# Second block's values and forget gate from split operands, and a reordered first block, in a two-block transformer kernel

## The reference, cut to what matters

```python
def reference(...):        # 512 tokens, width 1024
    x = first_block(x, mem, ...)     # one hybrid layer
    return second_block(x, ...)

def hybrid_layer(x, mem, ...):
    h = rmsnorm(x, norm_g);  proj = h @ w_in        # latents, conv parts, q_mem, gates, r
    q, k, v from rmsnorm(latents)                   # 8 heads, rope on the last 32 of 96
    o_attn = attention(q, k, v) * silu(g_attn)
    o_conv = c_b * short_conv(c_c * c_u) * silu(g_conv)
    mkv = rmsnorm(mem, mem_norm_g) @ w_mkv          # 256 memory rows
    o_mem = attention(rmsnorm(q_mem), rmsnorm(m_k), m_v) * silu(g_mem)   # 4 heads
    y = sum of sigmoid(r + b) * (o @ w_br) over the three branches
    return x + y @ w_out

def second_block(x, ...):
    xn = rms_norm(x, norm1_g);  proj = xn @ w_in    # fq fk fv, forget, dq dk dv
    8 causal heads with forget gates, 8 dilated heads; h = x + mixed @ w_out
    h = h + peer_ffn(rms_norm(h))                   # 16384 experts, top 16 of 8 heads
    return rms_norm(h)
```

## Time and profile before

| | |
|---|---|
| three runs | 2448.0, 2450.22, 2455.33 us; median 2450.22 us |
| the profiled execution | 2454.08 us, of which the span is 2452.2 us |
| PE matmul busy | 2312.9 us, 94% of the span |
| POOL, DVE, ACT busy | 1226.3, 1252.9, 898.9 us |
| mean granted PE clock | 0.978 of full speed |

### The profile page before, as it was taken

The page is one execution under the profiler, slowest core; times in us unless marked ns, Lnnn a source line. Parts: engine busy times, 40 slices in busy tenths (PEclk is TensorE's granted clock), DMA queues, the critical chain, the costliest instruction groups (busy, mean ns, idle before and its releaser), DMA issues.

```text
span 2452.2 us, 29634 instructions
## 1 busy us (share of the span) xinstructions
PE 2312.9 (94%) x9678; PEld 1770.4 (72%) x9678; DVE 1252.9 (51%) x2348; ACT 898.9 (37%) x1409; POOL 1226.3 (50%) x793
## 2 busy tenths in 40 slices
PE   7898999889998899899999999999999799999997
PEld 5565566568773566668888888888887688888886
DVE  2444434130521245529766676422221688888886
ACT  3445443343632244433333333322222333333332
POOL 3222022124530222134888888888888665555553
PEclk9999999999998999999999999999999899999999
DMA  6545122214621111123466666666656799999995
GB/s 215 172 158 173 61 84 87 78 56 124 202 84 52 65 39 44 34 87 87 78 147 144 144 145 149 142 146 145 118 106 115 270 320 349 355 357 351 356 352 211
DMA packets 229280, 392.31 MB, mean 160 GB/s; under 512 B 77616, under 2 KB 153392, under 8 KB 228944
## 3 DMA queue, kind: packets, MB, share of 16 engines
q1 hardware_dynamic: 150864, 323.89, 40.2%
q0 software_dynamic: 78336, 67.45, 13.8%
HBM read 330.21 MB, written 61.01 MB: 160 GB/s over the span
## 4 chain that ended last, share of the span: by engine, by line
PE 63%; issue 1%; DVE 1%; ACT 1%; DMA 0%; POOL 0%; DVEq 0%; ACTq 0%; SPq 0%; POOLq 0%
PE bank L1208 28%; PE bank L1219 21%; PE bank L1020 9%; PE bank L1149 2%; PE bank L1120 1%; PE bank L1187 1%; PE bank L1133 1%; PE bank L1072 0%; DVE low L1627 0%; ACT blocks L1422 0%; DVE h_low L1649 0%; DMA tail<-gates 0%; PE bank L1124 0%; ACT staged L1248 0%; PE bank L1197 0%
## 5 line engine op out<-in xcount | busy, mean ns | idle before, releaser
L913 POOL DMA_INDIRECT gates<-low x384 | 621.7, 1619 | 116.3 <-issue 115.8
L885 POOL TENSOR_TENSOR u_split<-blocks,u_split 128x1024 fp32r<-128x1024 f32 x106 | 259.0, 2444 | 825.0 <-ACT u_split L1331 824.4
L1208 PE MATMUL bank<-h_high,u_tiles_split 128*128 128x512 f32 x2048 | 631.3, 390 | 1.2 <-ACT low L1517 1.2
L1020 PE MATMUL bank<-h_high,u_split 128*128 128x512 f32 (+1 forms) x1696 | 570.1, 410 | 25.6 <-DVE h_low L1649 11.9
L1219 PE MATMUL bank<-v_split,a_split 128*128 128x512 f32 x2304 | 524.3, 391 | 15.2 <-DVE a_split L1920 15.2
L1219 PEld LDWEIGHTS bank<-v_split,a_split 128*128 128x128 f32 x2304 | 434.2, 188 | 105.2 <-DVE v_split L1917 15.6
L1208 PEld LDWEIGHTS bank<-h_high,u_tiles_split 128*128 128x128 f32 x2048 | 384.8, 188 | 80.8 <-ACT low L1517 1.4
L1020 PEld LDWEIGHTS bank<-h_high,u_split 128*128 128x128 f32 (+1 forms) x1696 | 324.8, 192 | 110.5 <-issue 28.6
L1208 PE MATMUL bank<-h_low,u_tiles_split 128*128 128x512 f32 x1024 | 399.0, 390 | 0.0
L1794 DVE TENSOR_TENSOR u_tiles_split<-tail,u_tiles_split 128x1024 fp32r<-128x1024 f32 x128 | 157.1, 1228 | 364.2 <-ACT u_tiles_split L1497 363.4
L1020 PE MATMUL bank<-h_low,u_split 128*128 128x512 f32 x720 | 284.8, 396 | 0.0
(11 more groups left out here) (181 smaller groups left out, 2330.5 us busy)
## 6 DMA issues: line engine op xcount, KB each, us to landing
tail<-in_uT SPq DMA_DIRECT2D x128, 512.0 KB, 3.8
tail<-in_v SPq DMA_DIRECT2D x128, 512.0 KB, 5.6
gates<-blocks SPq DMA_DIRECT2D x32, 768.0 KB, 5.8
tail<-gates SPq DMA_DIRECT2D x128, 192.0 KB, 5.5
kept_hidden<-tail SPq DMA_DIRECT2D x96, 192.0 KB, 1.9
tail<-kept_hidden SPq DMA_DIRECT2D x96, 192.0 KB, 5.6
blocks<-in_r SPq DMA_DIRECT2D x24, 512.0 KB, 4.0
blocks<-in_conv SPq DMA_DIRECT2D x16, 512.0 KB, 4.3
```

The costliest lines, as they stand in the source:

```text
L885: nc.gpsimd.tensor_tensor(flat(u, 1)[:, 0:n], ring[:, loads[0] % NW, 0:n], flat(u, 0)[:, 0:n].bitcast(F32), ALU.subtract).then_inc(s_wlo, 1)
L913: nc.gpsimd.indirect_dma_start(gate_elements, bass.IndirectOffsetOnAxis(ap=expert_no[tb][:, k:k + 1], axis=0), expert_gate[tb][:, k:k + 1] ...
L1020: last = mm(ps[0:m, :], flat(u, part)[:, k * m:(k + 1) * m], x, start=(k == 0 and j == 0), stop=(k == nk - 1 and j == 2))
L1208: last = mm(bank[slot % 2][:, :], U4[:, slot, w, k, :], x[:, k, :], start=(k == 0 and x is hh and w == 0), stop=(k == KD - 1 and w == 1))
```

## The change

The steps of the first block are put in another order, with one piece of work moved to another engine. The angles are made right behind the first norm. The second and later conv `post` steps come behind the next head's q and k instead of ahead of the last `W`. The squares of q and k become steps of their own between the `X` and `PV` steps. The squares of the memory rows go from ACT, with eight sums on PE, to POOL: eight squares and seven additions (`mem_squares`), one behind each of eight conv tiles, and one sum on PE. The memory heads get `r` tiles ahead of them, and the eight gate tiles come behind all of them, together with `split b`. `split y` is done behind every third branch tile. A weight slot that held a chunk of the memory values is released chunk by chunk.

In the second block `wf` and `v2` join `SPLIT`. `v2` becomes eight tiles, each with a quarter of the input features: it adds 6 matmuls to each of four banks, and behind the fourth and the eighth tile ACT copies the four banks. Norm `x2` makes the low parts of the activations as it goes. From the fourth `qk2` tile on, ACT splits the next weights behind the second `X` copy of the following head and no longer right behind the `qk2` tile's own copy.

```diff
...
         conv_ns.append(tile("conv", c, KD, P, True))
-        if c % 4 == 3:
-            post("conv", c // 4, conv_ns[-4:])
+        if 2 <= c < 2 + KD:
+            STEPS.append(("mem_squares", c - 2))
+        if c == 3:
+            post("conv", 0, conv_ns[-4:])
+        elif c % 4 == 3:
+            late.append((c // 4, conv_ns[-4:]))
+
+    late = []
+
+    def late_posts():
+        while late:
+            post("conv", *late.pop(0))
...
+    STEPS.append(("angles",))
...
-        yield lambda: (pre_q(h), pre_k(h), STEPS.append(("sq", f"q{h}")), STEPS.append(("sq", f"k{h}")))
+        yield lambda: (pre_q(h), pre_k(h))
+        yield lambda: STEPS.append(("sq", f"q{h}"))
+        yield lambda: STEPS.append(("sq", f"k{h}"))
         yield lambda: STEPS.append(("norm", f"q{h}"))
...
+        late_posts()
+        if h == 3:
+            STEPS.append(("norm", "mem"))
         columns(h, 0)
         columns(h, 1)
         more()
         STEPS.append(("PV", h, 0))
+        more()
         columns(h, 2)
         more()
         STEPS.append(("PV", h, 1))
+        more()
...
-        gate(2 * h)
-        gate(2 * h + 1)
+        filler()
+        filler()
         STEPS.append(("W", a, TB - 1))
-        if h >= 2:
-            STEPS.append(("split", "b", 4 * (h - 2), 4 * (h - 1)))
...
-    filler()
+    for i in range(8):
+        gate(i)
+        if i == 5:
+            STEPS.append(("split", "b", 0, 4))
     for i in range(4):
         post("mgate", i, [])
+    STEPS.append(("split", "b", 4, 8))
...
+        if j >= 3 and j % 3 == 0:
+            STEPS.append(("split", "y", j // 3 - 1, j // 3))
+    STEPS.append(("split", "y", KD - 1, KD))
...
     post("forget", 0, [tile("wf", 0, KD, 8, True)])
-    STEPS.append(("high_h", "x2"))
-    for g in range(2):
-        Ls = [load("v2", 4 * g + c, 1024) for c in range(4)]
-        for tb in range(TB):
-            proj("v2", TB * g + tb, Ls)
-    STEPS.append(("low_h",))
+    for i in range(8):
+        tile("v2", i, 2, T)
+    STEPS.append(("key_biases",))
...
-SPLIT = ("lat", "kpe", "conv", "gate", "qm", "r", "br", "wo", "qk2", "wo2", "wq")
+SPLIT = ("lat", "kpe", "conv", "gate", "qm", "r", "br", "wo", "wf", "v2", "qk2", "wo2", "wq")
...
+                    was, c, _ = LOADS[loads[0] - NW]
+                    by_chunk = was == "mv" and c < 3
+                    after = max(after, min(last_use[loads[0] - NW] + (not by_chunk), n - 1))
...
+                elif s[0] == "mem_squares":
+                    k, mm_, total = s[1], dtmp[:, MEM:2 * MEM], dtmp[:, 0:MEM]
+                    if k == 0:
+                        pool.wait_ge(s_mem, 16)
+                        pool.wait_ge(s_tab, 2)
+                    dst = mm_ if k else total
+                    nc.gpsimd.tensor_tensor(dst, memT[:, k, :], memT[:, k, :], ALU.mult).then_inc(s_msq, 1)
+                    if k:
+                        pool.wait_ge(s_msq, 2 * k)
+                        nc.gpsimd.tensor_tensor(total, total, mm_, ALU.add).then_inc(s_msq, 1)
+                        pool.wait_ge(s_msq, 2 * k + 1)
...
-                def normalised(k):
-
-                    if k < KD - 1:
-                        pe.wait_ge(s_hk, KD - 1 + k + 1)
-                    else:
-                        pe.wait_ge(s_norm, norm_no["x2"])
-                    return hT[:, k, :]
+                def values():
+
+                    u = unit[n]
+                    c = i % 4
+                    if i == 0:
+                        pe.wait_ge(s_Ph, x_no[(HEADS + MEM_HEADS - 1, MB - 1)])
+                        pe.wait_ge(s_O, O_no[HEADS + MEM_HEADS - 1])
+                    for tb in range(TB):
+                        if i == 4:
+                            if tb < TB - 1:
+                                pe.wait_ge(s_vfree, tb + 1)
+                            else:
+                                pe.wait_ge(s_evac, ev(pi[("v2", 3)]))
+                        for k in range(2):
+                            t = 2 * c + k
+                            if i < 4:
+                                pe.wait_ge(s_hl, parts0["x2"] + t + 1)
+                            for j, (part, x) in enumerate(((0, hh), (0, hl), (1, hh))):
+                                last = mm(bank[3 + tb][:, :], x[:, t, tb * P:(tb + 1) * P],
+                                          flat(u, part)[:, k * T:(k + 1) * T],
+                                          start=(t == 0 and j == 0), stop=(t == KD - 1 and j == 2))
+                        if c == 3 and tb < TB - 1:
+                            last.then_inc(s_vb, 1)
+                    return last
...
+                if key == "mem":
+                    i = auxi[("norm", key)]
+                    need_aux(i)
+                    pe.wait_ge(s_msq, 2 * nk - 1)
+                    mm(ax[i % 2][:, 0:MEM], ones, dtmp[:, 0:MEM], start=True, stop=True).then_inc(s_aux, 1)
+                    return
...
+                if kind == "v2":
+                    if i % 4 == 3:
+                        V = (VA, VB)[i // 4]
+                        for tb in range(TB):
+                            if tb < TB - 1:
+                                act.wait_ge(s_vb, (TB - 1) * (i // 4) + tb + 1)
+                            else:
+                                act.wait_ge(s_proj, n + 1)
+                            nc.scalar.copy(V[:, tb], bank[3 + tb][:, :].rearrange("p (h d) -> p h d", h=HEADS))\
+                                .then_inc(s_vfree if tb < TB - 1 else s_evac, 1)
+                    return
...
+            waiting = []
             for s in STEPS:
                 if s[0] == "proj":
                     evac(s[1])
-                    for u in split_after.get(s[1], []):
-                        high_weights(u)
+                    waiting += split_after.get(s[1], [])
+                    if PROJ[s[1]][0] != "qk2" or PROJ[s[1]][1] < 3:
+                        while waiting:
+                            high_weights(waiting.pop(0))
...
                     high_probs(s[1], s[2])
+                    if s[2] == 1:
+                        while waiting:
+                            high_weights(waiting.pop(0))
...
+                    if key in H_NO and k == KD - 1:
                         end(ins, s_norm, "s_norm")
-                    if key in ("x", "h2") and k > 0:
+                    if key in H_NO and k > 0:
                         low_h(key, k - 1)
-                if key in ("x", "h2"):
+                if key in H_NO:
...
-                elif s[0] == "low_h":
-                    for k in range(KD):
-                        if k < KD - 2:
-                            dve.wait_ge(s_chunk, 3 + k // 2 + 1)
-                        else:
-                            dve.wait_ge(s_proj, pi[("v2", 2 * TB - 1)] + 1)
-                        low_h("x2", k)
...
```

More of the change, by code:

```diff
@@ L173, in build_schedule @@
     fill = [lambda c=c: conv_part(c) for c in range(2, 16)]
[L174 to L175 removed]
+    fill += [lambda h=h: normed("qm", h) for h in range(MEM_HEADS)]
     fill += [lambda h=h: normed("mk", h) for h in range(MEM_HEADS)]
@@ L205, in columns @@
         STEPS.append(("L", a, kb))
-    for f in prep_mla(0):
+    for i, f in enumerate(prep_mla(0)):
         f()
-        filler()
+        if i not in (1, 2):
+            filler()
     rows(0)
@@ L628, in program, with ev @@
         for k in NORMS:
-            sq0[k] = n
-            n += norm_shape(k)[0]
+            if k != "mem":
+                sq0[k] = n
+                n += norm_shape(k)[0]
         pi = {(k, i): n for n, (k, i, _) in enumerate(PROJ)}
+        evacuated = [not (kind == "v2" and i % 4 < 3) for kind, i, _ in PROJ]
+        def ev(n):
+            return sum(evacuated[:n + 1])
         auxi, n = {}, 0
```

91 lines of the change are left out of this document (42 added, 49 removed).

## The result

The changed kernel takes 2381.1 us at the median of four runs (2377.0 to 2388.8), the kernel before 2451.6 (2448.0 to 2455.3). The ratio is 0.971, with a 95% interval of 0.969 to 0.974. That is 14 us above the forecast of 2367.4 and inside the range for all cases (2349 to 2389), but 3 us above the forecast's own range (2355 to 2378). The profiled run took 2388.84 us at a span of 2386.6, the slowest of its four.

A forecast was written before the change was run, and what follows sets the result against it. The prediction took PE, busy 94% of the span, to bound the kernel. Its terms sum to 82.8 us, from 2454.08 to 2371.3, less 3.9 for the median: 2367.4; own range 2355 to 2378, for all cases 2349 to 2389.

The forecast's parts named there:

- Angles, 10.0: First norm: angles no longer wait for ACT's cast; 8.1 us of PE waiting and 1.9 of lower clock saved.
- Heads 0 to 6, 13.3: First block's heads: 7.0 us from waits ahead of transposes, 3.0 of clock, 3.3 in heads 3 to 6 saved.
- memory norm, 3.8: Norm of the memory rows: PE's idling and 16 records give way to one matmul; 3.8 us saved.
- Memory heads 20.6: Memory heads: causes of eight PE waits leave, clock gained, handovers and one new 1.0 us stall stay; 20.6 us saved.
- split y 5.9: First output tile: PE's 3.12 us wait for low parts and 2.8 of lower clock go; 5.9 us saved.
- port and branches -2.0: Port and branch stage: squares hit DVE, and splits of y load ACT and DVE; 2.0 us lost, bounds 0 and 17.
- Forget gate -1.0: Norm x2 and forget gate, made as split matmuls: end at 754.5 against 753.5 us, a loss of 1.0.
- values 17.1: Second block's values: eight split tiles of 5.48 us, 43.8 instead of 60.9; 17.1 us saved.
- two qk2 tiles 8.1: First two qk2 tiles of the second block: second one's weights are ready, two take 11.0 us; 8.1 saved.
- Second-block heads, 7.0: Second block's heads: seven waits of about 1.06 us at the first PV go; 7.0 us saved, bounds 0 and 7.4.
- the clock doesn't come back: Rival, chance 0.09: shorter waits still bring PE's lower clock level, so 17 us are lost, giving 2384.
- POOL's squares cost: Rival, chance 0.15: POOL's squares and interleaved splits cost time in conv and branch tiles; 17 instead of 2.0, giving 2382.

The follow-up runs named there:

- angles_late: The changed kernel with the angles on DVE back behind ACT's cast; 2394.4 us, ratio 0.977 to the kernel before.
- few_after: The changed kernel without the last 16 of the 384 gate scatters, for timing only; 2361.9 us, ratio 0.964 to the kernel before.
- memsq_act: The changed kernel with the norm of memory as before: squares on ACT, eight sums on PE, none on POOL; 2381.6 us, ratio 0.972.
- sq_first: The changed kernel with head 0's squares of q and k ahead of the conv tile again; 2381.9 us, ratio 0.970.
- gates_back: The changed kernel with the eight gate tiles and their splits of b between the memory heads again; 2397.9 us, ratio 0.978.
- tidy: The changed kernel with head 0's squares ahead of the conv tile, and weight splits behind the copies for memory heads and third qk2 tile; 2377.4 us, ratio 0.969.
- no_defer: The changed kernel with the second block's weight splits again right behind each tile's copy on ACT; 2386.9 us, ratio 0.974.
- two_ops: The changed kernel with memory's norm as before, plus one multiply and one add on POOL at the start; 2394.3 us, ratio 0.977.

## Why the prediction was right and where it failed

The direction, the places and most of the sizes were right. That the time lies in the range is in part owed to the range, which takes in two rivals at 2382 and 2384: the forecast's own case left it out. Of the signs, two failed: PE waits 1.19 to 1.23 us in the memory heads where none over 0.6 was to be, and one first `PV` waits 1.29.

**Angles, 10.0.** 10.1 in the table, 9.9 by angles_late. The row of 8.67 us and the low clock behind it both went, as read from the earlier trace rows.

**Heads 0 to 6, 13.3, and memory norm, 3.8.** Together 16.7 in the profiled run and 19.6 in few_after. memsq_act splits the 16.7 into 10.2 and 6.6. The norm's term was too small, mostly by the 2.0 of waiting that the new order would have added. The heads' 13.3 counted 3.0 of clock as gained; few_after got that back (19.6 less 6.6 is 13.0) and the profiled run didn't. The waits that were to replace the old one are 0.24 us (at 138.04 and its like), not 0.5.

**Not in the sum: head 0.** "The post step itself (some 6 us of DVE) is next needed out of the way by the norm of q" was as far as the prediction looked at the new order of a head's preparation. In head 0 the squares of q and k had moved behind the conv tile's copy and weight split on ACT. PE waited 2.37 us, and where the clock fell behind it 1.6 to 3.1 more: 2.6 to 5.7 us, shown by sq_first.

**Memory heads 20.6, split y 5.9, port and branches -2.0.** 25.1 for 24.5, and this agreement is partly luck. Taken at the first and last branch matmul (609.26 and 681.58 before, 566.62 and 638.82 after) and the norm's first sum, it is 18.8 for the memory heads and gates, 6.2 for `split y`, and 0.1 for the branch tiles, so the loss of 2.0 did not come and made up for 1.8 too much in the heads. gates_back puts 15.5 on the gates' place. PE's waits ahead of the value products are 1.23 us each, where 0.25 was forecast: the "one new stall" of 1.0 is in every head, and tidy takes 4.3 us of it away.

**Forget gate -1.0, values 17.1, two qk2 tiles 8.1.** -0.9 and 25.6. Split matmuls with activations as the stationary side follow each other every 0.227 us (192 in 43.5), the price taken for them.

**Second-block heads, 7.0.** 7.3 between no_defer and few_after, from six waits and not the seven that were counted. In the profiled run 1.6: the clock was at its lower level where it had not been before, most of all at 762 to 773 us.

**The clock.** The rival "the clock doesn't come back" was given 0.09 as an alternative to the forecast. It is no alternative but a spread on top of it: the same program reached the u stage at 1116.0, 1125.7 and 1128.2 us. Some of the changed kernel's runs pay it and some don't, and the few us that the forecast counted as gained for certain are part of it.

**The step that failed: "The second half of the program has the same instructions before and after, and I let it cost the same."** The instructions are the same and their start moved by 75.2 us, but their time isn't. At its middle PE waits for POOL's scatters, 15.16 us before the change, 23.86 after (few_after). The scatters became slower by 8.9 us in all, and this came with the squares on POOL in the first block: without them the chain is at 746.2 us (memsq_act), and with one multiply and one add in their place at 758.8 again (two_ops). By which way they act stays open. So *POOL's squares cost* was the rival nearest to the truth in its price, 12.7 us of idle time between two_ops and memsq_act, and wrong in its mechanism and place: in the first 420 us DVE is busy 2.9 us longer than in memsq_act, and PE's conv tiles lose nothing. That this half was bound by POOL at one point stood in the trace of before, in a bracket of 15 us that I did not read, since I stopped at 860 us.

## What to carry to other kernels

Follow the trace to its end, even where the code is the same: a wait of 15 us in an untouched stage says that another engine's chain sets the time there, and such a chain passes an earlier start on to the stage behind it, and any slower pace of its own as well. Where PE idles at a meeting point, look for work that the late engine can give away: six splits moved from POOL to DVE gave more than all other repairs of this study together. And when an order is made by a generator, read the first pass of a loop apart from the others.

## What the hardware showed that I had not expected

One of these scatters, an indirect DMA of POOL, takes 1.55 us to issue, and 2.57 when it starts just behind a DVE instruction with two inputs in SBUF. From the timelines of POOL and DVE in the u stage of the changed kernel:

```profile
1697.04 1.56 POOL L946 DMA_INDIRECT gates<-low  x1 [0.30 <-issue]
1698.90 2.57 POOL L946 DMA_INDIRECT gates<-low  x1 [0.30 <-issue]
1701.77 1.56 POOL L946 DMA_INDIRECT gates<-low  x1 [0.30 <-issue]
```

```profile
1698.82 1.23 DVE L1864 TENSOR_TENSOR u_tiles_split<-tail,u_tiles_split 128x1024 fp32r<-128x1024 f32 x1 [4.21 <-ACT u_tiles_split L1575]
1704.26 1.23 DVE L1864 TENSOR_TENSOR u_tiles_split<-tail,u_tiles_split 128x1024 fp32r<-128x1024 f32 x1 [4.21 <-ACT u_tiles_split L1575]
```

The 1.02 us more is about the rest of DVE's instruction (1.15 us from the scatter's start to its end). The Trainium skill, SBUF — State Buffer, section "Who interferes with whom", says that a DVE instruction with two SBUF inputs contends with a GpSimd instruction that reads SBUF, and that the port pair they share is an exclusive lock. The trace agrees: the scatter reads the gates from SBUF. The same section says that in a probe `tensor_tensor` did not stall a DMA whose descriptors GpSimd makes; here it held up the issue of one, 2.57 us for 1.55, and the measurement decides.

Call a scatter that is held up so a hit. In the last 340 us of the chain the hits form a beat: three scatters take 5.57 us and a u tile 5.44, so POOL slips by 0.13 us per tile until one scatter is hit, which puts it back in step, mostly every sixth tile (hits at 621, 653, 686 and 719 us into the chain). At the median of 1.547 three take 5.54 and it is every seventh or eighth (583, 621, 659, 697).

This beat is the smaller part of what the slower pace costs. 9 ns more for each of 384 scatters are 3.5 us. What scatters take above their median adds up to 27.7 us before and 33.3 after. From 420 us into the chain on it is 7.0 and 8.8; between 120 and 420 us, where DVE's top-k search adds more two-input instructions of 1.23 us and the hits come in groups, it is 15.4 and 19.6 (11.7 in memsq_act, 19.7 in two_ops). Why the slower pace meets more of them there is not shown, and it isn't the pace alone: the kernel before and memsq_act have the same median, with chains of 749.9 and 746.2 us.
